# Attention interleaved with the k and v blocks, norms with a later split and an early table load, and stages begun on half the channels

## What is computed

```python
for i in range(DEPTH):
    hp, hs = _modulate(yp, shm_p, scm_p), _modulate(ys, shm_s, scm_s)    # adaLN: h = y * (1 + scale) + shift
    if i % 2 == 0:
        qp, kp, vp = _qkv(hp, attn_w_qkv[j]); qs, kq, vq = _qkv(hs, attn_w_qkv[j])
        mp = _moba_prompt(qp, kp, vp) @ attn_w_o[j]          # causal softmax attention with ALiBi
        ms = _moba_sample(qs, kq, vq, cache_k, cache_v, ...) @ attn_w_o[j]   # 256 cached positions + own
    else:
        mp, ms = conv module (two pointwise projections, depthwise conv of width 31, a norm)
    y = _layernorm(DEEPNORM_ALPHA * y + (1 + gate) * m, ...)
    f = _swiglu(h) if i % 2 == 0 else _moe(h)                # top 2 of 8 experts
    y = _layernorm(DEEPNORM_ALPHA * y + (1 + gate) * f, ...)
```

## Time and profile before

| | us |
|---|---|
| median of three runs (2002.76 to 2003.96) | 2003.96 |
| the profiled execution | 2008.72 |
| its span, from the first instruction to the last | 2007.0 |
| mean granted TensorE clock, as a share of 2.4 GHz | 0.946 |

### The profile page before, as it was taken

The page is one execution under the profiler, slowest core; times in us unless marked ns, Lnnn a source line. Parts: engine busy times, 40 slices in busy tenths (PEclk is TensorE's granted clock), DMA queues, the critical chain, the costliest instruction groups (busy, mean ns, idle before and its releaser), DMA issues.

```text
span 2007.0 us, 27233 instructions
## 1 busy us (share of the span) xinstructions
PE 1831.6 (91%) x10086; PEld 1471.7 (73%) x10086; DVE 1524.6 (76%) x1604; ACT 1168.8 (58%) x1030; POOL 18.1 (1%) x73
## 2 busy tenths in 40 slices
PE   5999778999899878998999999999999999999997
PEld 2974457999788766676676767676688787887885
DVE  2567736555679758989899898989888788887884
ACT  1321213443345327888877887877767767676773
POOL 2000000000000000000000000000000000000000
PEclk8985778999989888999999999999999999999998
DMA  9747677555743416999999999999999899898980
GB/s 299 230 149 238 245 251 252 168 174 182 240 141 104 175 39 245 382 385 388 388 390 394 380 388 386 381 386 390 387 330 366 324 338 370 304 357 337 329 314 22
DMA packets 246105, 579.27 MB, mean 289 GB/s; under 512 B 10478, under 2 KB 122550, under 8 KB 246013
## 3 DMA queue, kind: packets, MB, share of 16 engines
q1 hardware_dynamic: 245005, 573.98, 78.7%
q0 software_dynamic: 1024, 4.25, 0.6%
HBM read 574.79 MB, written 4.35 MB: 289 GB/s over the span
## 4 chain that ended last, share of the span: by engine, by line
PE 58%; DVE 16%; issue 7%; ACT 5%; DVEq 1%; DMA 0%; ACTq 0%; SPq 0%; PEldq 0%
PE banks L861 17%; PE banks L468 12%; DVE w_lo L1622 12%; PE banks L849 11%; PE banks L819 4%; ACT w_hi L1092 4%; PE banks L678 3%; PE banks L699 2%; PE banks L805 1%; PE banks L765 1%; PE banks L783 1%; PE banks L540 1%; PE banks L517 1%; PE banks L829 1%; PE banks L497 1%
## 5 line engine op out<-in xcount | busy, mean ns | idle before, releaser
L1622 DVE TENSOR_TENSOR w_lo<-ring,w_hi 128x2048 fp32r<-128x2048 f32 x420 | 945.6, 2288 | 146.0 <-ACT w_hi L1092 146.0
L1092 ACT CAST w_hi<-ring 128x2048 fp32r<-128x2048 f32 x420 | 798.7, 1912 | 265.9 <-PE banks L861 169.1
L861 PE MATMUL banks<-w_hi,x_s 128*128 128x512 f32 x672 | 279.3, 416 | 45.5 <-DVE w_lo L1622 39.6
L849 PE MATMUL banks<-w_hi,g_buf 128*128 128x512 f32 x784 | 282.5, 401 | 5.2 <-DVE w_lo L1622 2.8
L861 PE MATMUL banks<-w_hi,x_m 128*128 128x512 f32 x896 | 283.1, 392 | 2.3 <-DVE w_lo L1622 2.3
L468 PE MATMUL banks<-h_hi,w_hi 128*128 128x264 f32 x800 | 238.1, 298 | 29.5 <-DVEq L430 29.5
L861 PE MATMUL banks<-w_lo,x_s 128*128 128x512 f32 x672 | 264.7, 394 | 0.0
L982 ACT CAST w_hi<-ring 128x1024 fp32r<-128x1024 f32 x124 | 121.5, 1031 | 198.3 <-PE banks L468 93.0
L468 PE MATMUL banks<-h_lo,w_hi 128*128 128x264 f32 x800 | 233.9, 292 | 0.0
L468 PE MATMUL banks<-h_hi,w_lo 128*128 128x264 f32 x800 | 233.4, 292 | 0.0
L1245 DVE TENSOR_TENSOR w_lo<-ring,w_hi 128x1024 fp32r<-128x1024 f32 x124 | 143.9, 1204 | 106.0 <-ACT w_hi L982 105.2
(11 more groups left out here) (347 smaller groups left out, 1912.8 us busy)
## 6 DMA issues: line engine op xcount, KB each, us to landing
ring<-in_moe_w_dram SPq DMA_DIRECT2D x420, 1024.0 KB, 7.4
ring<-in_ada_w_dram SPq DMA_DIRECT2D x48, 1024.0 KB, 5.9
ring<-in_ffn_w_dram SPq DMA_DIRECT2D x30, 1024.0 KB, 5.5
ring<-in_attn_w_qkv_dram SPq DMA_DIRECT2D x12, 1024.0 KB, 11.9
ring<-in_conv_w_pw_dram SPq DMA_DIRECT2D x12, 1024.0 KB, 9.7
ring<-in_cache_k_dram SPq DMA_DIRECT2D x16, 512.0 KB, 6.0
ring<-in_cache_v_dram SPq DMA_DIRECT2D x16, 512.0 KB, 7.5
ring<-in_attn_w_o_dram SPq DMA_DIRECT2D x4, 1024.0 KB, 8.5
```

The source lines that it names most:

```text
L849: mm = pe.matmul(out_b[:, b, :], g, y, start=(p == 0 and t == 0 and i == 0), stop=(p == NCH - 1 and t == 2 * last + 1 and i == len(g_passe ...
L861: mm = pe.matmul(bk[:, b, :], x, y, start=(k == 0 and i == 0), stop=(k == KC - 1 and i == len(x_passes(k, hi, lo)) - 1), skip_group_check= ...
L1092: act.copy(w_unit(n)[0], ring[:, pos_of(n), :]).then_inc(ev("moe_hi_ready"), 1)
L1622: dve.tensor_tensor(lo, ring[:, pos_of(n), :], hi.bitcast(F32), ALU.subtract).then_inc(ev("moe_lo_ready"), 1)
```

## The change

Three things. **Order of attention:** the four q blocks come first; then eight turns, each with one k or v block (`KV` = k0, v0, k1, v1, ...), the attention of the chunks whose k and v are there, pages of cached keys (`PAGES_AT`: two sequences in each of the first two turns, then one, none in the last two) and an adaLN filler. The order of loads follows; w_o blocks 0 and 1 are loaded in turns 6 and 7, ahead of the cached values. ACT instead of VectorE copies the k and v blocks and their transposes (`keep`), and VectorE passes the drain on (`kept`). The attention's operand gets a place of its own (`attn_hi`, `attn_lo`); the samples' part moves to the end of the turns and uses the banks of the norms. **Half channels:** `dense_halves` runs two blocks on channel chunks 0 to 3 and then 4 to 7, each half behind its `h_lo`; used for q blocks 0 and 1, f1 and f3 block 0, p1 and p1g block 0, and p2 blocks 0 and 1. **Norms:** ACT does a square root of one column first, and the split behind the last block comes behind the centring.

```diff
+        PAGES_AT = ((0, 1), (2, 3), (4,), (5,), (6,), (7,), (), ())
         for c in range(KC):
+            if c + 2 < KC:
+                qkv_block(KV[c + 2])
+            else:
+                wo_block(c + 2 - KC)
+            for n in PAGES_AT[c]:
+                pages(("K", n), cache_k[0], n, "dve")
             ada(*fillers[c])
...
+            def dense_halves(i, slots, x_hi, x_lo, behind=None):
+                for s in slots:
+                    wait_split(s)
+                groups = [(s, m, group((s, m))) for s in slots for m in range(2)]
+                for half in range(2):
+                    pe.wait_ge(ev("h_lo_ready"), 2 * i + half + 1)
+                    for s, m, bk in groups:
+                        for k in range(4 * half, 4 * half + 4):
+                            hi, lo = halves(s, k, m)
+                            for n, (w, x) in enumerate(((hi, x_hi), (hi, x_lo), (lo, x_hi))):
+                                mm = pe.matmul(bk[:, 0:T], w, x[:, k, :], start=(k == 0 and n == 0),
+                                               stop=(k == KC - 1 and n == 2), skip_group_check=True)
+                        if half:
+                            filled(mm)
+                for s in slots:
+                    freed[split_no[s]] = (psum_filled, len(order))
...
-            pe.wait_ge(ev("h_ready"), 1)
-            dense([("qkv", j) for j in range(12)], h_hi, h_lo)
+            dense_halves(0, [("qkv", j) for j in range(2)], h_hi, h_lo)
+            dense([("qkv", j) for j in range(2, 4)], h_hi, h_lo)
...
+            for n in range(KC):
+                g, is_v = divmod(n, 2)
+                blk = ("qkv", KV[n])
+                dense([blk], h_hi, h_lo)
+                if n >= 1:
+                    scores(n - 1)
+                for i in PAGES_AT[n]:
+                    q_all(i)
+                if n == KC - 1:
+                    self_scores()
+                filler()
+                kept((blk, 1))
+                if is_v:
+                    turn_pair("v_tok", hT[:, :, :], g)
+                else:
+                    turn_pair("k_tok", qkT[:, KC:, :], g)
+                if n >= 2:
+                    attend(n - 2)
+                if n == KC - 2:
+                    kept(("k_tok", g))
+                    turn("k_s", lambda c: qkT[:, KC + c, TP:T], NS, 2)
...
+            scores(KC - 1)
             ada_turn()
+            turn("v_s", lambda c: hT[:, c, TP:T], NS, 2)
             pe.wait_ge(ev("sample_probs_ready"), 1)
...
+            attend(KC - 2)
             pe.wait_ge(ev("sample_probsT_ready"), 1)
-            pv = [group(("pv_s", half)) for half in range(2)]
+            pv = [stat, stat2]
...
+                if e == 0:
+                    attend(KC - 1)
...
-            pe.wait_ge(ev("h_ready"), 2)
-            for j in range(FF // 256):
+            dense_halves(1, [("f1", 0), ("f3", 0)], h_hi, h_lo)
+            while pending:
+                ada_turn()
+            for j in range(1, FF // 256):
                 dense([("f1", j), ("f3", j)], h_hi, h_lo)
...
             def norm(i, z, s):                                   (ACT)
+                act.activation(warm[:, 0:1], eps_t[:, 0:1], ACT.Sqrt)
...
+            for n in range(KC):                                  (ACT)
+                for m in range(2):
+                    keep((blk, m), hT[:, 2 * g + m, :] if is_v else qkT[:, KC + 2 * g + m, :], lambda bk: bk[:, 0:T])
+                split_behind(blk)
...
+                if n >= 2:
+                    attend(n - 2)
+                if n >= 1:
+                    exps(n - 1)
+                if n >= 2:
+                    keep_attention(n - 2)
...
             def modulate(i, layer, k):                           (VectorE)
                 for half in range(2):
+                    if half:
+                        low_halves(i, 0)
...
-                for half in range(2):
-                    low_halves(i, half)
+                low_halves(i, 1)
...
             def rstd_ready(i, z, behind=None):                   (VectorE)
...
+                if behind is not None:
+                    split_behind(behind)
                 dve.wait_ge(ev("ln_std_ready"), i + 1)
...
+            for n in range(KC):                                  (VectorE)
+                if n >= 2:
+                    normalise(n - 2)
+                kept((blk, 0))
+                kept((blk, 1))
+                if n >= 1:
+                    scores(n - 1)
+                for i in PAGES_AT[n]:
+                    sample_scores(i)
...
+                filler()
+                split_behind(blk)
+                kept(("v_tok" if is_v else "k_tok", g))
+                if n >= 2:
+                    attend(n - 2)
...
+            normalise(KC - 2)
+            scores(KC - 1)
+            ada_turn()
+            sample_rows("v_s", v_s)
```

More of the change, by code:

```diff
@@ L307, in build @@
             pages(("V", n), cache_v[0], n, "pe")
-        for j in range(4):
-            block(("wo", j), w_o, j * 256)
+        for j in range(2, 4):
+            wo_block(j)
         for j in range(FF // 256):
@@ L592, in scores, with self_scores, attend @@
                     filled(pe.matmul(bk[:, :], ident[0:NS, c:c + 1].to_broadcast([NS, P]), q_s[:, half * 512:(half + 1) * 512], start=True, stop=True))
[L594 to L598, removed]
+            def self_scores():
+                pe.wait_ge(ev("self_scores_ready"), 1)
+                bk = group("self_s")
+                filled(pe.matmul(bk[:, 0:H], e8T[:, :], ss[:, :], start=True, stop=True))
+            def attend(c):
                 for hh in range(2):
@@ L611, in _ @@
                 filled(mm)
-            ada_turn()
[L614 to L621, removed]
+            for n in range(KC):
[19 more added lines that the diff above has]
+                    turn("k_s", lambda c: qkT[:, KC + c, TP:T], NS, 2)
+                    pe.wait_ge(ev("sample_scores_ready"), 1)
+                    bk = group("scores_s")
+                    for i in range(PAGES):
+                        mm = pe.transpose(bk[:, i * P:(i + 1) * P], scT[:, i, :], ident[:, :])
+                    filled(mm)
+            scores(KC - 1)
+            ada_turn()
+            turn("v_s", lambda c: hT[:, c, TP:T], NS, 2)
             pe.wait_ge(ev("sample_probs_ready"), 1)
@@ L986, in split_behind @@
                 q = split_no[name] + AHEAD
-                if q < len(splits) and not (name[0] == "qkv" and splits[q][0] == "wo"):
+                if q < len(splits):
                     split(splits[q])
@@ L1001, in _, with keep @@
             operand(0)
-            for j in range(12):
+            for j in range(4):
                 split_behind(("qkv", j))
+            def keep(name, dst, src):
+                act.copy(dst, src(see(name))).then_inc(ev("act_kept"), 1)
             def exps(c):
@@ L1413, in sample_scores, with normalise @@
                     settle()
-            scores(0)
-            sample_scores(0)
-            for c in range(KC):
+            def normalise(c):
                 for hh in range(2):
@@ L1454, in _, with sample_rows @@
-            settle()
-            step(dve.tensor_scalar(s_self[:, 3:4], s_self[:, 2:3], -0.125, None, ALU.mult))
-            announce("sample_max_ready")
+                drained(dve.tensor_tensor(attn_lo[:, c, 0:TP], bk[:, 0:TP], attn_hi[:, c, 0:TP].bitcast(F32), ALU.subtract))
+            def sample_rows(name, rows_s):
+                for half in range(2):
+                    bk = take((name, half))
+                    drained(dve.tensor_copy(rows_s[:, half * 512:(half + 1) * 512], bk[0:NS, :]))
+                announce(name[0] + "_ready")
```

206 lines of the change are left out of this document (114 added, 92 removed).

## The result

The changed kernel takes **2011.14 us** (median; 2007.38 to 2014.01), the kernel before 2006.97 beside it (2002.55 to 2009.62): ratio 1.0023, 95% interval 1.0014 to 1.0032. The forecast was 1989, faster. The profiled execution after took 2014.01 with a span of 2012.3; before it was 2008.72 and 2007.0. So the span is 5.3 us longer, and three stretches make it up: 18.2 won up to the end of w_o, 10.5 lost behind the norms, and 12 to 13 lost in the experts, whose code the change doesn't touch.

The account below looks back on a forecast made before the run. Attention was bound by neither slow-clocked TensorE nor VectorE alone, plus a serial tail. 20.8 us won there less 6.2 lost at the norms gave 14.6, from 2003.96 to 1989; own range 1978 to 1998, 8-in-10 range 1968 to 2004.

Parts of the forecast that it names:

- The rest, experts included, only moves: Everything outside attention and norms, experts included: shifts in time only, with no gain or loss of its own.
- the one that ended slower: Rival, 10 in 100: in the loop small matmuls keep TensorE near 1.2 GHz, turns take 22.8 us, the whole 2015.
- first half blocks: Start of q blocks 0 and 1 on half of the channels: at 57.4 us instead of 52.98, 4.5 later.
- the stop: Behind q blocks 0 and 1, which end together: TensorE stands 3.5 us for cast and split of block 2.
- block 3: Fourth k or v block of the attention loop: claimed to start at 139.2 us.
- the wait for the adaLN load: Loop turn 1: adaLN loads issued only behind the split at 109.3; TensorE through its turn at about 122 us.
- cycles: Loop turns 3 to 5: 15.3 us each by PSUM drains, 18.0 if the block starts slow; 17 taken.
- The rival that the clock stays up: Rival, 18 in 100: blocks keep TensorE at 2.4 GHz through the attention loop, turns take 15.3 us, the whole 1973.
- Late start of f1: First norm: TensorE, waiting for four PSUM groups, begins f1 and f3 at 328.2 us, 1.0 later than before.
- Next block: f1 block 1, behind the first pair: begins 6.3 us after its end instead of 3.5, 2.9 more lost.
- The third norm: Norm ahead of p2: start 1.6 us late, but a net loss of only 0 to 0.5, 0.3 taken.
- p2 block 2 begins where it did: Behind the third norm: the second block comes ahead of the adaLN turns, so block 2 starts no later than before.

Follow-up runs that it names:

- e2: The changed kernel with warm put into an unused column of prm instead of a tensor of its own: 1998.23 us, ratio 0.9969.
- e8: e4 with the K pages spread one to a turn, but two in turn 1: 1978.39 us, ratio 0.986.
- e4: e3 with q, too, begun on all channels, blocks 0 and 1 one after the other: 1978.85 us, ratio 0.9881.
- e7: e4 with the start on half of the channels for one block at a time, only its own two banks taken ahead: 1966.53 us, ratio 0.9793.
- e3: e2 with the three stages behind norms begun on all channels, q still on halves: 1985.77 us, ratio 0.9906.
- e6: The kernel before with w_hi and w_lo 32 bytes higher and everything behind them 64 bytes higher: 2019.03 us, ratio 1.006.
- e10: The kernel before with w_hi and w_lo 32 bytes higher and everything behind them 128 bytes higher: 2018.89 us, ratio 1.0069.
- e13: The kernel before with w_hi, w_lo and everything behind them 32 bytes higher together: 2005.53 us, ratio 1.0002.

## Why the prediction was wrong, step by step

**The step that failed** is the last sentence of the sum, "The rest, experts included, only moves". It was put down without a term: one new tensor and two wider ones stood in the diff, and their addresses were not looked at. The experts add 12.2 to 12.7 (offset -7.7 at their start, +4.5 to +5.0 at their end), some 11 of it by the placement, and that makes the sign. The sum said -14.6; measured without the experts it is -7.7, and e2, at 1998 inside the range, wins 6.2. So even with the placement put right less than half of the forecast gain is there: attention and norms, below, miss in the same direction. No rival had it: the one that ended slower put its loss into the loop's clock, which rose. The Trainium skill (SBUF — State Buffer, section "Operand start alignment") asks only for a multiple of the element's size and says that this is about legality, not speed; all placements here obey it, and their times differ by 0.6%.

**Attention: mechanism right in the main, 3.8 short.** 20.8 forecast, 17.0 measured (17.6 by the means above, with traces of the kernel before spread over 6 us). Terms, forecast and measured: first half blocks 57.4 and 59.01 (the modulation started 1.5 later, at 48.19 instead of 46.73, behind an adaLN load; but the first q block of the kernel before starts anywhere from 52.9 to 54.9 in the eight traces); the stop 3.5 and 3.6; loop 89.5 and 91.81; block 3 139.2 and 146.57. Here the wait for the adaLN load was placed right and sized short: the split ended at 112.04 instead of 109.3, the load landed at 124.69, then came the rest of an adaLN row (1.93), an adaLN turn (1.81) and transposes (0.94) at the lower clock, and block 2 took 7.23, where the sum had full speed. From block 3 to block 6 it was 51.0 and 52.3, with cycles of 15.96, 19.6 and 16.75 (forecast 17 each); block 6 to w_o 66.7 and 61.9, a tail that ran better than taken. In the first and third of these cycles the chain goes through VectorE's copy of the adaLN row, as the sum had it. In the second TensorE is busy for 19.0 of 19.6 us at a clock of 0.69 and sets the beat itself. In e8 block 3 started 6.0 us earlier than in e4 and w_o did not, so how much of the 7.4 reached the end is open.

The rival that the clock stays up came true in its cause (0.89) and not in its time: at a clock of 1.00 the cycle took 15.96, 0.7 over its 15.3, at 0.95 16.75 and at 0.69 19.6. The rule of the Trainium skill that was weighed (TensorE: Matmul & The Clock Gate, "HAM oscillation") would have made all three 18.0: two of three stayed below 17, and one took 19.6.

**Norms: reason for the late start right, 4.3 short.** 6.2 forecast, 10.5 measured. That halves can't start early because four banks are taken first is shown: the second adaLN copy releases TensorE at 310.20, and e7, with two banks, starts early. Late start of f1: 1.0 forecast, 1.2. Next block 2.9 later forecast, 4.6 measured: the third and fourth adaLN turn waited as the sum had it, 4.5 us from the end of the pair (323.53 to 328.03), but ran at 1.2 GHz then and took 3.55 instead of 1.8; at full clock all four had taken 3.47. The pair itself ran 0.5 shorter than before. FFN at a lower clock 1 and 1.05, p1 1.0 and 1.2. The third norm is a mis-sized term, 0.3 against 1.8. Chain from the first p2 matmul, before and then after:

```profile
685.40 8.14 PE banks L468 x48
693.54 3.52 PE banks L497 x32
697.06 4.51 PE banks L468 x24
```

```profile
677.28 14.01 PE banks L499 x96
...
692.18 3.47 PE banks L531 x32
695.65 4.55 PE banks L481 x24
```

"p2 block 2 begins where it did" came true: its first matmul comes 42.6 us behind the last tap, 42.2 before. But the half block behind the adaLN turns runs at a low clock, 4.51 us at 0.65 before and 4.55 at 0.63 after, where one at full clock takes 2.90. Before, that was block 1; now it is block 2, and the sum left it out. TensorE runs without a stop from the start of p2 to its end, 32.9 us before and 33.0 after, so that the late start stays late. Up to the last tap another 0.8 was lost behind p1, where the sum said that others waited already. The shortened norm itself gave 0.7 (21.05 before, 20.36 in e3, from w_o to f1): 0.6 had been forecast.

**q: right in its sum.** e4 gives back 6.9 of the 8.0 that the start on halves was to cost. The stop of 3.6 goes as forecast; the start gains 2.5 of 4.5, as said at e4.

## What to carry to other kernels

When a diff adds or widens a tensor, compare the addresses of both operands of the long matmul loops before and after, and keep their distance; a 4-byte tensor turned 0.3% faster into 0.2% slower, and a spare column of an existing tensor avoided it. Take accumulators as late as you can: work that could start on half of its input waits for the last bank that is claimed ahead of its first instruction. What moves earlier must be followed to its consumer: ten microseconds at block 2 were worth nothing at w_o, and two blocks that end together expose a split that had been hidden.

## What the runs showed of the hardware that was not expected

In the large items (x_m, g_buf) a matmul of 512 columns starts 227 ns (median) after the one before it when weights and columns lie a multiple of 256 bytes apart in their partition, and 229 to 241 ns after it at 32, 64, 96 and 128 bytes beyond one (tenth to ninetieth percentile; medians 232 to 235), whether the addresses themselves are multiples of 128 or odd multiples of 32. In the small items (x_s) the step is less clean: median 231 before, with a quarter of the starts at 236 and more, and 235 after.

Matmuls of 264 columns show the same in another form. In the dense blocks the columns move on by 1056 bytes for each k and the weights by 1024, so the distance walks through eight values, 0 to 224 in steps of 32. The median gaps between starts, three for each k, worked out from the trace's start times, were 121, 116, 120 for k = 0, 120, 124, 119 for k = 1 and 129, 120 for k = 7 before. With w_hi and w_lo 32 bytes higher (e6; e10 and e13 agree to 1 ns or so) they were 129, 120, 122 for k = 0, then 121, 115, 120 for k = 1 and 121, 124, 119 for k = 2: the same pattern one k later. The sum of the 23 gaps of a group is 2.78 us in both, and so the dense blocks lost nothing.
